# Mixer weights split once, kept in memory, and loaded as pairs by the later blocks of a hybrid encoder block

## The chip, the cores and the metric

One core of one Trainium2 chip runs the whole kernel. The metric is the device time of one execution in microseconds (us). Engines: PE is TensorE, DVE VectorE, ACT ScalarE, POOL GpSimd, SP SyncE, which only issues DMAs here.

## What is computed

One layer of a streaming encoder on 4096 frames of width 1024, in float32, with 16 meta tokens ahead of them:

```python
h = layernorm(concat([meta, x]), ln0)
proj = h @ w_in                      # q k v, conv cb cc ch, gates ga gc
y_attn = window_attention(q, k, v, sinks) @ w_attn_out
y_conv = (cb * conv3(cc * ch)) @ w_conv_out
mix = (sigmoid(ga) * y_attn + sigmoid(gc) * y_conv) @ w_o
h = layernorm(alpha * h + mix, ln1)
h = layernorm(alpha * h + top2_of_32_experts(h), ln2)
```

The change is in the mixer, which is the part up to `mix` and `ln1`.

## The kernel before

**Float32 by halves.** A float32 product on PE is made of three products of rounded parts: high by high, high by low, low by high (`product`, lines 826 to 828). So each weight needs a high part, `w_hi`, and a low part, `w_lo`.

**Blocks and strips.** The mixer works through 8 blocks of 512 frames (`BLOCKS`), one pass of a loop on every engine for each. A block is 50 strips (`N`); a strip is 128 x 1024 weights, 512 KB. Their order is the list `strips` (lines 85 to 90): k, v, four q (strips 0 to 5), then cc, ch, cb four times (6 to 17), then ga, gc, out eight times (18 to 41; `MIX0` is 18), then eight of w_o (42 to 49). Each strip is 24 matmuls of 512 columns. Between the strips PE does the attention of the block (in strips 6 to 15), the router of the block before it (18 to 24) and transposes.

**The way of a strip's weights.** SP loads it into `raw`, which has five places (`load`, line 451: it waits for `lo_ready`, that is for the split of the strip that had the place, so it runs some four strips ahead of the other engines). ACT rounds it to `w_hi` (`split_hi`, line 513), when PE has done with the place of `w_hi`; DVE subtracts to get `w_lo` (`split_lo`, line 656); PE waits for `lo_ready` and multiplies. `w_hi` and `w_lo` have two places each. All this is done again in each of the 8 blocks.

**Counts.** PE adds 1 to `strip_done` at the last matmul of each strip (`mm.then_inc(strip_done, 1)`), and DVE adds 2 at the start (`v.sem_inc(strip_done, 2)`). So `strip_done >= b * N + s + 3` means that strip s of block b is finished.

**The outputs.** Each strip writes one of two banks of PSUM (`pj`) in turn; an out strip writes both, one after the other. PE waits for `pj_taken` before it writes a bank again. ACT empties those of ga and gc (`take`), DVE those of out (lines 764 to 775): line 767 the first bank, line 769 the second.

**The input rows of the next block.** `x_rows` has four tiles of 128 frames. In SP's program a tile's load is issued at steps 26 to 29 (`X_AT`, `MIX0 + 8 + i`), behind the weight load of the same step (line 473). In DVE's program the wait for the tile and its statistics (`measure`, lines 41 to 44) are at steps 26, 29, 32 and 35 (`LN0_AT`), ahead of all else of that step:

```python
X_AT = {MIX0 + 8 + i: i for i in range(TILES)}
LN0_AT = {MIX0 + 8 + 3 * i: i for i in range(TILES)}
...
if s in LN0_AT:
    v.wait_ge(x_in[LN0_AT[s]], b * 16 + 16)
    measure(b * LNS + TILES + LN0_AT[s], LN0_AT[s], xs)
```

At steps 1 to 4 DVE does the statistics of ln1 on the rows of the block before, POOL scales them, and SP stores them at steps 4 to 7, twice (`h1`, 512 KB each).

After the mixer come the routing and the experts, which the change leaves alone.

Of the kernel before, what the change touches and what calls it, by code (L numbers as in the profile page):

```python
# [12 lines left out]
P = 128  # L13
# [40 lines left out]
def mixer(nc, t, x, w_in, w_attn_out, w_conv_out, w_o, h1, logits):  # L54
# [37 lines left out]
    RAW = 5  # L92
    assert N % RAW == 0 and N % 2 == 0
# [35 lines left out]
    with ExitStack() as ctx:  # L129
# [6 lines left out]
        raw = sb("raw", [P, RAW, D])  # L136
        w_hi = sb("w_hi", [P, 2, D], F32R)
        w_lo = sb("w_lo", [P, 2, D], F32R)
# [34 lines left out]
        arena = sb("arena", [P, 2 * KD * TOK])  # L173

        def place(at, name, shape, dt=FP32):
            size = 4 * math.prod(shape[1:])
            assert at[0] + size <= shared + 4 * 2 * KD * TOK
            placed = nc.alloc_sbuf_tensor_at(name, shape, dt, offset=at[0])
            at[0] += size
            return placed  # L180

# [27 lines left out]
        with ExitStack() as c1, nc.Block() as block:  # L209
# [4 lines left out]
            raw_in = [sem1(f"meta_raw_in{i}") for i in range(RAW)]  # L214
# [20 lines left out]
            @block.sync  # L235
            def _(sp):
                def load_strip(n):
                    for dst, src in strip_dmas(*meta_strips[n], raw[:, n % RAW, :]):
                        sp.dma_start(dst, src).then_inc(raw_in[n % RAW], 16)
# [6 lines left out]
                for n in range(1, RAW):  # L246
# [12 lines left out]
                for n in range(RAW, len(meta_strips)):  # L259
                    sp.wait_ge(pj_ready, n - RAW + 1)  # L260
                    load_strip(n)
                sp.wait_ge(consts_in, 16 * (7 + TAPS))
# [104 lines left out]
            @block.tensor  # L367
            def _(pe):
                pe.wait_ge(ident_ready, 1)
                pe.wait_ge(ln_done, 1)  # L370
                for k in range(KD):
                    mm = pe.transpose(tp[0][:, k * META:(k + 1) * META], hm[:, k * P:(k + 1) * P],
                                      ident[0:META, 0:META])
                mm.then_inc(tp_ready, 1)
                uses = [0] * RAW
                for what, n in order:
                    if what == "rows":
                        pe.wait_ge(ln_done, n + 1)
                        for half in range(2):
                            q = 2 * (n - 1) + half  # L380
                            pe.wait_ge(tp_taken_dve, max(1, q))
                            for k in range(4):
                                mm = pe.transpose(tp[q % 2][:, k * P:(k + 1) * P],
                                                  xs[:, n - 1, (4 * half + k) * P:(4 * half + k + 1) * P], ident[:, :])
                            mm.then_inc(tp_ready, 1)
                        continue
                    kind, i = meta_strips[n]
                    uses[n % RAW] += 16 * len(strip_dmas(kind, i, raw[:, 0, :]))
                    pe.wait_ge(raw_in[n % RAW], uses[n % RAW])
                    if n == 0:  # L390
                        pe.wait_ge(tp_taken_dve, 1)
                    if n >= 2:
                        pe.wait_ge(pj_taken, n - 1)
                    for k in range(KD):
                        mm = pe.matmul(pj[n % 2][:, 0:META], raw[:, n % RAW, k * P:(k + 1) * P], hmT[:, k, :],
                                       start=(k == 0), stop=(k == KD - 1))
                    mm.then_inc(pj_ready, 1)
# [4 lines left out]
        h1_out = [sem(f"h1_out{i}") for i in range(TILES)]  # L402
        hi_ready = sem("hi_ready")
# [37 lines left out]
        def raw_uses(s, b):  # L441

            per = lambda ss: 16 * len(strip_dmas(*strips[ss], raw[:, 0, :]))
            slot = s % RAW
            in_block = sum(per(q) for q in range(slot, N, RAW))
            return b * in_block + sum(per(q) for q in range(slot, s + 1, RAW))

        with nc.Block() as block:
            @block.sync
            def _(sp):  # L450
                def load(s, b):

                    hold(sp, lo_ready, b * N + s + 1)
                    for dst, src in strip_dmas(*strips[s % N], raw[:, s % RAW, :]):
                        sp.dma_start(dst, src).then_inc(raw_in[s % RAW], 16)

                load(0, 0)
                with sp.Fori(0, BLOCKS) as b:
                    for s in range(N):
                        load(s + 1, b)  # L460
# [7 lines left out]
                        if s in X_AT:  # L468
# [4 lines left out]
                            sp.dma_start(xs[:, i1, :], x[bass.ds(nxt * TOK + i1 * P, P), :]).then_inc(x_in[i1], 16)  # L473
                for i1 in range(TILES):
# [37 lines left out]
            def _(a):  # L512
                def split_hi(b, s):
                    uses = raw_uses(s, b) if s < N else raw_uses(0, b + 1)
                    a.wait_ge(raw_in[s % RAW], uses)
                    a.wait_ge(strip_done, b * N + s + 1)
                    a.activation(w_hi[:, s % 2, :], raw[:, s % RAW, :], ACT.Copy).then_inc(hi_ready, 1)  # L517
# [30 lines left out]
                split_hi(0, 0)  # L548
                with a.Fori(0, BLOCKS) as b:
                    for s, (kind, i) in enumerate(strips):  # L550
# [30 lines left out]
                        split_hi(b, s + 1)  # L581
# [15 lines left out]
                        if s in HX_AT:  # L597
# [4 lines left out]
                             .then_inc(hx_hi, 1)  # L602
                for i in range(TILES):
# [6 lines left out]
            def _(v):  # L610
# [19 lines left out]
                def take_logits(b, block_of):  # L630
# [7 lines left out]
                v.sem_inc(lo_ready, RAW)  # L638
# [5 lines left out]
                v.wait_ge(hi_ready, 1)  # L644
                v.tensor_tensor(w_lo[:, 0, :], raw[:, 0, :], w_hi[:, 0, :].bitcast(FP32), ALU.subtract)\
                 .then_inc(lo_ready, 1)
                with v.Fori(0, BLOCKS) as b:
# [7 lines left out]

                    def split_lo(s):
                        v.wait_ge(hi_ready, b * N + s + 1)
                        v.tensor_tensor(w_lo[:, s % 2, :], raw[:, s % RAW, :], w_hi[:, s % 2, :].bitcast(FP32),  # L658
                                        ALU.subtract).then_inc(lo_ready, 1)
# [18 lines left out]
                    for s, (kind, i) in enumerate(strips):  # L678
# [29 lines left out]
                        if 0 <= n < UNITS:  # L708
# [24 lines left out]
                        split_lo(s + 1)  # L733
# [68 lines left out]
                    assert steps[0] == DVE_STEPS  # L802
                v.wait_ge(wo_taken, BLOCKS * 2 * TILES + 1)
# [19 lines left out]
            def _(pe):  # L823
# [35 lines left out]
                with pe.Fori(0, BLOCKS) as b:  # L859
                    pe.wait_ge(hx_lo, b * 2 * TILES + 1)  # L860
                    for s, (kind, i) in enumerate(strips):
# [27 lines left out]
                        pe.wait_ge(lo_ready, b * N + RAW + s + 1)  # L889
# [3 lines left out]
                        if kind == "wo":  # L893
# [5 lines left out]
                            for tt in range(TILES):  # L899
# [3 lines left out]
                                for k in range(2):  # L903
                                    w = slice(k * TOK, (k + 1) * TOK)
                                    mm = product(quad[tt][:, :], mT_hi[:, 2 * kk + k, toks], mT_lo[:, 2 * kk + k, toks],
                                                 w_hi[:, s % 2, w], w_lo[:, s % 2, w],
# [5 lines left out]
                        else:  # L912
# [4 lines left out]
                            for part, (x_hi, x_lo, k0, ks) in enumerate(parts):  # L917
                                no = out_no[(s, part)]
                                pe.wait_ge(pj_taken[no % 2], b * (NOUT // 2) + no // 2 + 1)
                                for k in range(ks):  # L920
                                    w = slice((k0 + k) * P, (k0 + k + 1) * P)
                                    mm = product(pj[no % 2][:, :], w_hi[:, s % 2, w], w_lo[:, s % 2, w],
# [54 lines left out]
                        if s in HX_AT:  # L977
# [8 lines left out]
                            mm.then_inc(hx_ready, 1)  # L986
                pe.wait_ge(hx_lo, BLOCKS * 2 * TILES + 1)
# [677 lines left out]
```

## Time and profile before

| | us |
|---|---|
| three runs | 4330.54, 4335.98, 4336.49 |
| median | 4335.98 |
| the profiled execution, its own time | 4333.28 |
| its span, first to last instruction | 4331.5 |
| of this the mixer's 8 blocks, 62 to 2691 us | 2629 |
| PE busy over the span | 4171.0 (96%) |
| DVE busy | 2518.7 (58%) |
| ACT busy | 1773.0 (41%) |

The difference between 4333.28 and 4331.5 is what lies around the span. Matmuls are pipelined: a row gives 390 to 400 ns for one of 512 columns, but they start some 227 ns apart. PEld is PE's weight load, which overlaps. "Idle before" is the time that the engine stood still ahead of such an instruction, and what ended it; "issue" means that nothing in the profile ended it. SPq is SP's queue, where DMAs are issued. Where two rows of DVE seem to overlap by some 0.1 us, the end of the first is its last write.

### The profile page before, as it was taken

The page shows a single profiled execution, that of the slowest core. Times are in us where ns is not written, and L with a number is a line of the kernel's source. Part 1 is how long each engine was busy: PE and PEld are TensorE (multiplying, and loading weights), DVE is VectorE, ACT ScalarE, POOL GpSimd, SP SyncE. Part 2 cuts the span into 40 slices and gives each one's busy share as a digit, 9 for nine tenths or more (in the row PEclk, how much of TensorE's full clock was granted, in tenths as well). Part 3 has the DMA queues.
Part 4 walks back from the last instruction along what each step waited for, and adds up shares of the span by engine and source line. Part 5 has one row for each costly group of instructions (what it writes and reads, how often), then busy time and mean ns, then how long its engine had stood idle before and what let it go on. Part 6 is the DMA issues. An engine that isn't in the chain of part 4 may idle for free. (4 is left out here: it accounts for less than half of the span.)

```text
span 4331.5 us, 62892 instructions
## 1 busy us (share of the span) xinstructions
PE 4171.0 (96%) x20252; PEld 3428.8 (79%) x20253; DVE 2518.7 (58%) x3263; ACT 1773.0 (41%) x2950; POOL 1094.6 (25%) x1117
## 2 busy tenths in 40 slices
PE   7999999999999999999999999499999999999997
PEld 7887887887887888888888887388788888778886
DVE  5555555555555655645645645777666666765664
ACT  2422422422422422422422422466555555654553
POOL 4022032022022021121121121134333333333333
PEclk9999999999999999999999999799999999999998
DMA  6333333333333333333332332187666666765562
GB/s 171 85 107 103 93 102 98 99 104 97 102 104 89 107 106 85 107 104 89 111 102 80 117 102 78 54 289 248 246 199 198 206 199 234 251 203 198 194 204 90
DMA packets 569472, 601.49 MB, mean 139 GB/s; under 512 B 104080, under 2 KB 426640, under 8 KB 569248
## 3 DMA queue, kind: packets, MB, share of 16 engines
q1 hardware_dynamic: 521152, 476.88, 35.5%
q0 software_dynamic: 48096, 121.71, 8.4%
q8 instruction: 130, 2.13, 0.2%
q14 instruction: 94, 0.77, 0.1%
HBM read 527.15 MB, written 124.78 MB: 151 GB/s over the span
## 5 line engine op out<-in xcount | busy, mean ns | idle before, releaser
L826 PE MATMUL bank<-hT_hi,w_hi 128*128 128x512 f32 x2176 | 864.8, 397 | 30.1 <-DVE w_lo L658 21.3
L658 DVE TENSOR_TENSOR w_lo<-raw,w_hi 128x1024 fp32r<-128x1024 f32 x400 | 597.3, 1493 | 485.5 <-ACT w_hi L517 484.4
L827 PE MATMUL bank<-hT_lo,w_hi 128*128 128x512 f32 x2176 | 850.6, 391 | 2.4 <-issue 2.4
L828 PE MATMUL bank<-hT_hi,w_lo 128*128 128x512 f32 x2176 | 849.2, 390 | 0.0
L1565 PE MATMUL e_bank<-e_w_hi,e_xT_hi 128*128 128x512 f32 x1312 | 521.9, 398 | 14.2 <-DVE e_xT_lo L1488 12.4
L826 PEld LDWEIGHTS bank<-hT_hi,w_hi 128*128 128x128 f32 x2176 | 408.9, 188 | 140.4 <-DVE w_lo L658 32.6
L1567 PE MATMUL e_bank<-e_w_hi,e_xT_lo 128*128 128x512 f32 x1312 | 514.3, 392 | 0.0
L1566 PE MATMUL e_bank<-e_w_lo,e_xT_hi 128*128 128x512 f32 x1312 | 513.4, 391 | 0.0
L1493 DVE TENSOR_TENSOR e_w_lo<-e_raw,e_w_hi 128x1024 fp32r<-128x1024 f32 x384 | 444.4, 1219 | 117.7 <-ACT e_w_hi L1441 110.8
L828 PEld LDWEIGHTS bank<-hT_hi,w_lo 128*128 128x128 f32 x2176 | 408.9, 188 | 87.4
L827 PEld LDWEIGHTS bank<-hT_lo,w_hi 128*128 128x128 f32 x2176 | 409.3, 188 | 86.6 <-issue 5.4
L517 ACT ACTIVATE w_hi<-raw 128x1024 fp32r<-128x1024 f32 x401 | 421.1, 1050 | 12.5 <-PE bank L828 7.9
L1441 ACT ACTIVATE e_w_hi<-e_raw 128x1024 fp32r<-128x1024 f32 x384 | 374.7, 1054 | 18.6 <-DMA e_raw<-in_w_exp_gate_dram 11.1
L1565 PEld LDWEIGHTS e_bank<-e_w_hi,e_xT_hi 128*128 128x128 f32 x1312 | 248.0, 189 | 67.4 <-issue 18.0
L1567 PEld LDWEIGHTS e_bank<-e_w_hi,e_xT_lo 128*128 128x128 f32 x1312 | 247.8, 189 | 53.4
L49 POOL TENSOR_SCALAR rstd<-moments 128x1 f32<-128x1 f32 (+1 forms) x73 | 43.5, 596 | 968.6 <-DVE moments L44 968.6
L1566 PEld LDWEIGHTS e_bank<-e_w_lo,e_xT_hi 128*128 128x128 f32 x1312 | 248.3, 189 | 49.7
L503 POOL COPY h_rows<-x_rows 128x1024 f32<-128x1024 f32 x32 | 33.4, 1044 | 986.7 <-PE bank L838 986.7
L1565 PE MATMUL e_bank<-e_w_hi,e_aT_hi 128*128 128x512 f32 x664 | 266.6, 401 | 2.8 <-DVE e_both L1502 2.7
L1567 PE MATMUL e_bank<-e_w_hi,e_aT_lo 128*128 128x512 f32 x664 | 260.2, 392 | 0.0
L1566 PE MATMUL e_bank<-e_w_lo,e_aT_hi 128*128 128x512 f32 x664 | 259.6, 391 | 0.0
L540 ACT ACTIVATE work<-bank 128x512 f32<-128x512 f32 x128 | 76.6, 599 | 427.6 <-PE bank L828 427.6
(277 smaller groups left out, 7173.3 us busy)
## 6 DMA issues: line engine op xcount, KB each, us to landing
raw<-in_w_in_dram SPq DMA_DIRECT2D x251, 512.0 KB, 3.9
e_raw<-in_w_exp_gate_dram SPq DMA_DIRECT2D x128, 512.0 KB
e_raw<-in_w_exp_up_dram SPq DMA_DIRECT2D x128, 512.0 KB
e_raw<-in_w_exp_down_dram SPq DMA_DIRECT2D x128, 512.0 KB
h_rows<-h_rows SPq DMA_DIRECT2D x72, 512.0 KB, 3.5
raw<-in_w_o_dram SPq DMA_DIRECT2D x64, 512.0 KB, 3.8
raw<-in_w_in_dram SPq DMA_DIRECT2D x64, 256.0 KB, 3.7
raw<-in_w_attn_out_dram SPq DMA_DIRECT2D x64, 256.0 KB, 2.8
```

Source lines behind the costliest of these rows:

```text
L49: po.tensor_scalar(rstd[0:rows, :], moments[0:rows, 1:2], LN_EPS, None, ALU.add).then_inc(ln_rstd, 1)
L517: a.activation(w_hi[:, s % 2, :], raw[:, s % RAW, :], ACT.Copy).then_inc(hi_ready, 1)
L540: a.activation(w[:, 0:TOK], got, ACT.Sigmoid).then_inc(taken_act, 1)
L658: v.tensor_tensor(w_lo[:, s % 2, :], raw[:, s % RAW, :], w_hi[:, s % 2, :].bitcast(FP32), ALU.subtract).then_inc(lo_ready, 1)
L826: pe.matmul(out, hi, x_hi, start=first, stop=False)
L827: pe.matmul(out, hi, x_lo, start=False, stop=False)
L828: return pe.matmul(out, lo, x_hi, start=False, stop=last)
L1441: a.activation(w_hi[:, c, :], raw[:, c, :], ACT.Copy).then_inc(split_count(e, c, True)[0], 1)
L1493: v.tensor_tensor(w_lo[:, c, :], raw[:, c, :], w_hi[:, c, :].bitcast(FP32), ALU.subtract)\
L1565: pe.matmul(out_p, hi, x_hi, start=first, stop=False)
L1566: pe.matmul(out_p, hi, x_lo, start=False, stop=False)
L1567: return pe.matmul(out_p, lo, x_hi, start=False, stop=last)
```

## The change

Block 0 is written out ahead of the loop, and the loop runs over blocks 1 to 7. In block 0 each strip is split as before, but two strips ahead, into one of three slots that hold high and low parts together (1 MB); SP stores the slot to memory (`split_weights`, 50 MB). `raw` has three places there. In blocks 1 to 7 SP loads strips from that tensor into four slots, three strips ahead, and nothing is split. SP's step s waits for `strip_done` there, where it waited for `lo_ready`. The rest of SP's step, the stores of h1 and the loads of x, stays behind that wait. The branch for block 0 in DVE's program goes, and a wait for `mlo_ready` comes in at the out strips.

```diff
-    RAW = 5
+    RAW, META_RAW = 3, 5
+    SLOTS = 4
+    ahead = RAW
+    slot_of = list(range(SLOTS)) * 5 + [0, 1, 2] + list(range(SLOTS)) * 6 + [0, 1, 2]
+    def first_slot(s):
+        return (s + 1) % RAW
...
-                def load(s, b):
-                    hold(sp, lo_ready, b * N + s + 1)
-                    for dst, src in strip_dmas(*strips[s % N], raw[:, s % RAW, :]):
+                def load_raw(s):
+                    if s >= RAW:
+                        sp.wait_ge(lo_ready, s - RAW + 1)
+                    for dst, src in strip_dmas(*strips[s], raw[:, s % RAW, :]):
                         sp.dma_start(dst, src).then_inc(raw_in[s % RAW], 16)
...
+                def store_split(s):
+                    sp.wait_ge(lo_ready, s + 1)
+                    sp.dma_start(split_d[s], slots[first_slot(s)]...).then_inc(w_out[first_slot(s)], 16)
+                def load_split(s, b):
+                    sp.wait_ge(w_out[first_slot(s)], ...)
+                    sp.dma_start(slots[slot_of[s]]..., split_d[s]).then_inc(w_in[slot_of[s]], 16)
...
-                load(0, 0)
-                with sp.Fori(0, BLOCKS) as b:
+                def block_of_loads(b, first):
                     for s in range(N):
-                        load(s + 1, b)
+                        if first:
+                            store_split(s)
+                        if first and s + ahead < N:
+                            load_raw(s + ahead)
+                        else:
+                            hold(sp, strip_done, b * N + s + 3)
...
+                            load_split((s + ahead) % N, b + (s + ahead) // N)
                         if s - 3 in LN1_AT:
...
                         if s in X_AT:
...
                             sp.dma_start(xs[:, i1, :], x[bass.ds(nxt * TOK + i1 * P, P), :]).then_inc(x_in[i1], 16)
...
-                        split_hi(b, s + 1)
+                        if first and s + 2 < N:
+                            split_hi(s + 2)
...
-                            if n == 1:
-                                with v.If(b == 0):
-                                    v.tensor_copy(bias[0:CHUNK, :, META:PREV], bias_prev[:, :, :])\
-                                     .then_inc(prev_set, 1)
+                            if n == 1 and first:
+                                v.tensor_copy(bias[0:CHUNK, :, META:PREV], bias_prev[:, :, :]).then_inc(prev_set, 1)
                                 v.wait_ge(prev_set, 1)
...
-                        split_lo(s + 1)
+                        if first and s + 2 < N:
+                            split_lo(s + 2)
...
+                            if i or not first:
+                                v.wait_ge(mlo_ready, b * KD + i)
...
-                        pe.wait_ge(lo_ready, b * N + RAW + s + 1)
+                        if first:
+                            pe.wait_ge(lo_ready, s + 1)
+                            w_of = slots[first_slot(s)]
+                        else:
+                            pe.wait_ge(w_in[slot_of[s]], w_uses(s, b))
+                            w_of = slots[slot_of[s]]
```

On ACT, DVE and PE the body of the loop becomes a function too, called once for block 0 and once in a loop from 1 to `BLOCKS`.

## Rows read from the trace of the kernel before

**Rows 1.** Stretches of one block: PE, PEld, DVE, ACT, POOL busy, clock, DMA, GB/s
```profile
core 0: us, PE busy (x) PEld busy (x) DVE busy (x) ACT busy (x) POOL busy (x), PEclk, DMA share, GB/s
62.00:391.00 329.00, 325.23 (x1611) 267.59 (x1612) 179.31 (x241) 108.98 (x198) 60.13 (x36) 1.00 0.37 104
...
2362.00:2691.00 329.00, 324.54 (x1612) 266.10 (x1612) 179.77 (x242) 106.23 (x196) 60.99 (x36) 1.00 0.31 92
```

**Rows 2.** Costliest groups of the page: busy us, mean ns, idle before
```profile
L658 DVE TENSOR_TENSOR w_lo<-raw,w_hi 128x1024 fp32r<-128x1024 f32 x400 | 597.3, 1493 | 485.5 <-ACT w_hi L517 484.4
L517 ACT ACTIVATE w_hi<-raw 128x1024 fp32r<-128x1024 f32 x401 | 421.1, 1050 | 12.5 <-PE bank L828 7.9
```

**Rows 3.** Waits of PE and PEld from 60 to 2730 us: total, times, longest
```profile
PE bank L826 <- DVE w_lo L658: 21.3, 20, 1.3
...
PEld bank L826 <- DVE w_lo L658: 32.6, 31, 1.6
```

**Rows 4.** Order of time, PE at strip 7 and DVE at a block's start
```profile
1094.58 0.50 PE L826 MATMUL bank<-hT_hi,w_hi 128*128 128x512 f32 x1 [1.26 <-DVE w_lo L658]
...
1379.66 0.20 DVE L676 COPY kT<-kT 128x64 f32<-128x64 f32 x1 [2.25 <-issue]
```

**Rows 5.** Order of time, PE between strips 26 and 27, DVE and ACT behind strips
```profile
1246.17 0.40 PE L828 MATMUL bank<-zT_hi,w_lo 128*128 128x512 f32 x1
1246.41 0.40 PE L826 MATMUL bank<-hT_hi,w_hi 128*128 128x512 f32 x1
...
1246.61 0.69 DVE L769 TENSOR_TENSOR work<-bank,work 128x512 f32<-128x512 f32 x1 [2.04 <-PE bank L828]
...
1252.09 0.60 ACT L540 ACTIVATE work<-bank 128x512 f32<-128x512 f32 x1 [2.44 <-PE bank L828]
1257.53 0.60 ACT L540 ACTIVATE work<-bank 128x512 f32<-128x512 f32 x1 [3.89 <-PE bank L828]
```

**Rows 6.** DMA queues of the page: packets, MB, share; and the 40 slices
```profile
q1 hardware_dynamic: 521152, 476.88, 35.5%
q0 software_dynamic: 48096, 121.71, 8.4%
...
GB/s 171 85 107 103 93 102 98 99 104 97 102 104 89 107 106 85 107 104 89 111 102 80 117 102 78 54 289 248 246 199 198 206 199 234 251 203 198 194 204 90
```

**Rows 7.** First matmuls of strips 4 and 8 of block 3, order of time
```profile
1071.72 0.39 PE L826 MATMUL bank<-hT_hi,w_hi 128*128 128x512 f32 x1
...
1102.05 0.50 PE L826 MATMUL bank<-hT_hi,w_hi 128*128 128x512 f32 x1
```

**Rows 8.** Order of time, SP's queue, steps 26 and 27 of block 3
```profile
1210.41 0.37 SPq L455 DMA_DIRECT2D raw<-in_w_in_dram  x1
1211.20 0.95 SPq L473 DMA_DIRECT2D x_rows<-in_x_dram  x1
1218.78 0.37 SPq L455 DMA_DIRECT2D raw<-in_w_in_dram  x1
1219.48 0.36 SPq L473 DMA_DIRECT2D x_rows<-in_x_dram  x1
```

**Rows 9.** Order of time, DVE at step 26 of block 3
```profile
1237.67 0.69 DVE L41 BATCH_NORM_STATS2 stats<-x_rows 128x6 f32<-128x512 f32 x1
1238.27 0.68 DVE L42 BATCH_NORM_STATS2 stats<-x_rows 128x6 f32<-128x512 f32 x1
1239.05 0.21 DVE L44 BATCH_NORM_AGGREGATE moments<-stats 128x2 f32<-128x12 f32 x1
...
1243.88 0.69 DVE L767 TENSOR_TENSOR work<-bank,work 128x512 f32<-128x512 f32 x1
```

**Rows 10.** DMA issues of the page's answer: KB each, us to landing
```profile
raw<-in_w_in_dram SPq DMA_DIRECT2D x251, 512.0 KB, 3.9
x_rows<-in_x_dram SPq DMA_DIRECT2D x32, 512.0 KB, 4.8
x_rows<-in_x_dram SPq DMA_DIRECT2D x1, 2048.0 KB, 11.8
```

**Rows 11.** Order of time, PE behind the 7.51 us that precede block 0
```profile
62.66 0.79 PE L826 MATMUL bank<-hT_hi,w_hi 128*128 128x512 f32 x1 [7.51 <-DVE w_lo L645]
...
66.66 0.44 PE L826 MATMUL bank<-hT_hi,w_hi 128*128 128x512 f32 x1
66.94 0.39 PE L827 MATMUL bank<-hT_lo,w_hi 128*128 128x512 f32 x1
```

**Rows 12.** Order of time, PE behind a shorter gap in the experts
```profile
3054.03 1.12 PE L1611 MATMUL e_bank<-e_ident,e_prod 128*128 128x128 f32 x4 [2.62 <-DVE e_prod L1542]
```

**Rows 13.** The stretch behind that gap, columns as in rows 1
```profile
3054.00:3060.20 6.20, 5.48 (x14) 4.20 (x15) 5.95 (x7) 6.20 (x8) 1.65 (x2) 0.50 0.49 163
```

More of the change, by code:

```diff
@@ L91, in mixer @@
     N = len(strips)
-    RAW = 5
-    assert N % RAW == 0 and N % 2 == 0
+    RAW, META_RAW = 3, 5
+    SLOTS = 4
+    ahead = RAW
+    slot_of = list(range(SLOTS)) * 5 + [0, 1, 2] + list(range(SLOTS)) * 6 + [0, 1, 2]
+    assert N == len(slot_of)
+    def first_slot(s):
+        return (s + 1) % RAW
     CONV0 = 2 + PAIRS
@@ L134, in sem @@
             return ctx.enter_context(nc.semaphore(name))
-        raw = sb("raw", [P, RAW, D])
-        w_hi = sb("w_hi", [P, 2, D], F32R)
-        w_lo = sb("w_lo", [P, 2, D], F32R)
+        split_d = nc.dram_tensor("split_weights", [N, P, 2 * D], FP32).ap()
         xs = sb("x_rows", [P, TILES, D])
@@ L180, in place @@
             return placed
+        at = [weights]
+        slots = [place(at, f"w_slot{i}", [P, 2, D], F32R) for i in range(SLOTS)]
+        raw = place([weights + 4 * 6 * D], "raw", [P, RAW, D])
+        meta_raw = place([weights + 4 * 4 * D], "meta_raw", [P, META_RAW, D])
         at = [shared]
@@ L213, in mixer @@
             gains_in = sem1("gains_in")
-            raw_in = [sem1(f"meta_raw_in{i}") for i in range(RAW)]
+            raw_in = [sem1(f"meta_raw_in{i}") for i in range(META_RAW)]
             ln_step, ln_moments, ln_rstd, ln_gained, ln_done = (
@@ L237, in load_strip @@
                 def load_strip(n):
-                    for dst, src in strip_dmas(*meta_strips[n], raw[:, n % RAW, :]):
-                        sp.dma_start(dst, src).then_inc(raw_in[n % RAW], 16)
+                    for dst, src in strip_dmas(*meta_strips[n], meta_raw[:, n % META_RAW, :]):
+                        sp.dma_start(dst, src).then_inc(raw_in[n % META_RAW], 16)
                 sp.dma_start(hm, t["meta"]).then_inc(meta_in, 16)
@@ L245, in _ @@
                 sp.dma_start(xs[:, :, :], x[0:TOK, :].rearrange("(t p) d -> p t d", p=P)).then_inc(x_in, 16)
-                for n in range(1, RAW):
+                for n in range(1, META_RAW):
                     load_strip(n)
@@ L258, in _ @@
                     sp.dma_start(dst, row.unsqueeze(0).to_broadcast([P, row.shape[0]])).then_inc(consts_in, 16)
-                for n in range(RAW, len(meta_strips)):
-                    sp.wait_ge(pj_ready, n - RAW + 1)
+                for n in range(META_RAW, len(meta_strips)):
+                    sp.wait_ge(pj_ready, n - META_RAW + 1)
                     load_strip(n)
@@ L374, in _ @@
                 mm.then_inc(tp_ready, 1)
-                uses = [0] * RAW
+                uses = [0] * META_RAW
                 for what, n in order:
@@ L387, in _ @@
                     kind, i = meta_strips[n]
-                    uses[n % RAW] += 16 * len(strip_dmas(kind, i, raw[:, 0, :]))
-                    pe.wait_ge(raw_in[n % RAW], uses[n % RAW])
+                    uses[n % META_RAW] += 16 * len(strip_dmas(kind, i, meta_raw[:, 0, :]))
+                    pe.wait_ge(raw_in[n % META_RAW], uses[n % META_RAW])
                     if n == 0:
@@ L394, in _ @@
                     for k in range(KD):
-                        mm = pe.matmul(pj[n % 2][:, 0:META], raw[:, n % RAW, k * P:(k + 1) * P], hmT[:, k, :],
+                        mm = pe.matmul(pj[n % 2][:, 0:META], meta_raw[:, n % META_RAW, k * P:(k + 1) * P], hmT[:, k, :],
                                        start=(k == 0), stop=(k == KD - 1))
@@ L402, in mixer @@
         h1_out = [sem(f"h1_out{i}") for i in range(TILES)]
+        w_in = [sem(f"w_in{i}") for i in range(SLOTS)]
+        w_out = [sem(f"w_out{i}") for i in range(RAW)]
         hi_ready = sem("hi_ready")
@@ L439, in mixer, with raw_uses, w_uses @@
         LNS = 2 * TILES
[L441 to L446, printed above, removed]
+        def raw_uses(s):
+            return sum(16 * len(strip_dmas(*strips[q], raw[:, 0, :])) for q in range(s % RAW, s + 1, RAW))
+        def w_uses(s, b):
+            slot = slot_of[s]
+            return 16 * ((b - 1) * slot_of.count(slot) + slot_of[0:s + 1].count(slot))
         with nc.Block() as block:
@@ L473, in _ @@
                             sp.dma_start(xs[:, i1, :], x[bass.ds(nxt * TOK + i1 * P, P), :]).then_inc(x_in[i1], 16)
+                for s in range(ahead):
+                    load_raw(s)
+                block_of_loads(0, True)
+                with sp.Fori(1, BLOCKS) as b:
+                    block_of_loads(b, False)
+                for s in range(ahead):
+                    sp.wait_ge(w_in[slot_of[s]], w_uses(s, BLOCKS))
                 for i1 in range(TILES):
@@ L512, in _, with split_hi @@
             def _(a):
[L513 to L517, printed above, removed]
+                def split_hi(s):
+                    a.wait_ge(raw_in[s % RAW], raw_uses(s))
+                    if s >= RAW:
+                        a.wait_ge(strip_done, s - RAW + 3)
+                        a.wait_ge(w_out[first_slot(s)], 16 * (sum(first_slot(q) == first_slot(s) for q in range(s))))
+                    a.activation(slots[first_slot(s)][:, 0, :], raw[:, s % RAW, :], ACT.Copy).then_inc(hi_ready, 1)
                 def take(b, s):
@@ L546, in take_rows, with block_of_strips @@
                      .then_inc(rt_act, 1)
-                split_hi(0, 0)
-                with a.Fori(0, BLOCKS) as b:
+                def block_of_strips(b, first):
                     for s, (kind, i) in enumerate(strips):
@@ L602, in _ @@
                              .then_inc(hx_hi, 1)
+                for s in range(2):
+                    split_hi(s)
+                block_of_strips(0, True)
+                with a.Fori(1, BLOCKS) as b:
+                    block_of_strips(b, False)
                 for i in range(TILES):
@@ L643, in _, with split_lo, block_of_strips @@
                 v.sem_inc(hx_lo, 1)
[L644 to L647, printed above, removed]
+                def split_lo(s):
+                    slot = slots[first_slot(s)]
+                    v.wait_ge(hi_ready, s + 1)
+                    v.tensor_tensor(slot[:, 1, :], raw[:, s % RAW, :], slot[:, 0, :].bitcast(FP32),
+                                    ALU.subtract).then_inc(lo_ready, 1)
+                def block_of_strips(b, first):
                     steps = [0]
@@ L802, in _ @@
                     assert steps[0] == DVE_STEPS
+                for s in range(2):
+                    split_lo(s)
+                block_of_strips(0, True)
+                with v.Fori(1, BLOCKS) as b:
+                    block_of_strips(b, False)
                 v.wait_ge(wo_taken, BLOCKS * 2 * TILES + 1)
@@ L857, in router_logits, with block_of_strips @@
                     mm.then_inc(lg_ready, 1)
-                with pe.Fori(0, BLOCKS) as b:
+                def block_of_strips(b, first):
                     pe.wait_ge(hx_lo, b * 2 * TILES + 1)
@@ L887, in _ @@
                             mm.then_inc(s_ready, 1)
[L889 removed]
+                        if first:
+                            pe.wait_ge(lo_ready, s + 1)
[3 more added lines that the diff above has]
+                            w_of = slots[slot_of[s]]
                         if kind == "out" and i == 0:
@@ L986, in _ @@
                             mm.then_inc(hx_ready, 1)
+                block_of_strips(0, True)
+                with pe.Fori(1, BLOCKS) as b:
+                    block_of_strips(b, False)
                 pe.wait_ge(hx_lo, BLOCKS * 2 * TILES + 1)
```

20 lines of the change are left out of this document (12 added, 8 removed).

## The prediction

> **What bounds the kernel now.** I read the stretches of single blocks first, since the change touches only the mixer. A block takes 329 us and PE is busy for 325 of them, at the full granted clock; DVE is busy for 179, ACT for 108, and the DMA engines move about 100 GB/s [rows 1]. Every one of the 8 blocks looks like this. So the mixer is bound by PE, and less work for DVE and ACT is worth only what PE waits for them. The costliest groups say that the splits are 597.3 us of DVE and 421.1 us of ACT [rows 2]; those are the large numbers of this change, and nearly all of them lie beside PE. The waits say what does not: PE stood still for `w_lo` 20 times in the mixer, 21.3 us in all, and its weight load 31 times, 32.6 us [rows 3]. These are some 3 or 4 places in each block: strip 1, where DVE is late because its loop begins again, strip 5 behind the layernorm work, and strip 7, where the split stands behind the preparation of the first scores (1.26 us in the row) [rows 4].
>
> **What is taken away.** In blocks 1 to 7 no `w_lo` is made, so these waits go; in block 0 the split is made two strips ahead, which gives it a strip of 5.44 us more (the two ends of ga and gc strips in [rows 5] are that far apart), and the waits are 1.6 us at most. Matmul rows overlap (0.39 us for one that starts every 0.23), so the PE figure is short by up to 0.16 us a time and the PEld figure holds some of its normal gaps. I take the middle, **27 us gained**, with 21.3 and 32.6 as ends. What could be late next at these places is DVE's preparation of scores or ACT's exponentials; both come sooner once their engines split nothing, so I take nothing off. The other 7/8 of 597.3 and 421.1 us are worth 0: PE's own work hides them.
>
> **Block 0.** SP now moves 0.5 MB in and 1 MB out for each strip; over a block of 329 us that is 79 MB or 240 GB/s, and slices at 248 and 289 GB/s stand in the page [rows 6]. A store has two strips and a raw load three before anyone needs it, so I take 0 (up to 10 us if that cover fails once). `raw` has three places for five, which is still three strips of lead. In block 0 SP's step waits for a split that is made two steps ahead of DVE's own step, so its loads of x are early enough.
>
> **The loads of blocks 1 to 7.** 1 MB for each strip of 5.44 us or more is at most 193 GB/s. The bytes that a busy DMA system moves follow from the queues: 476.88 MB in 35.5% of 4331.5 us is 310 GB/s for the mixed packets of q1, and 121.71 MB in 8.4% is 334 GB/s for the large ones of q0 [rows 6]. At 334 GB/s a slot of 1.05 MB takes 3.1 us, and its load is issued when PE ends strip s for use at strip s + 3, two strips or 10.9 us later. So the weights arrive in time: 0. At steps 4 to 7 two stores of 0.5 MB are behind each load, 2.1 MB or 6.3 us a strip; strips 4 to 7 together take PE 30.3 us, from 1071.72 to 1102.05 [rows 7], which is more than 4 times 6.3: 0.
>
> **What is moved: the loads of x.** This is the large term. SP's step 26 issues the weight load and then tile 0 of x. Today it is released by a split far back: in block 3 x was issued at 1211.20 [rows 8] and DVE measured it at 1237.67 [rows 9], 26 us later. After the change step 26 waits for `strip_done >= b * N + 29`, which is the end of strip 26 itself. But DVE's step 26 begins with the wait for that very tile, and only behind it, in order, comes line 767, which empties the first bank of strip 26. PE needs this bank for strip 27. So PE comes to a stop at the end of strip 26 until x has been asked for, has landed and has been measured. Nothing deadlocks, since strip 26 itself needs only what ACT has emptied. The length:
> - from the end of strip 26 to SP's first issue 0.1 us, as DVE follows the last matmul of strip 26 (1246.17 and 0.40) by less than that [rows 5].
> - from that issue to x landed: today x is issued 0.70 to 0.79 us behind the raw load [rows 8] and lands 4.8 us later [rows 10], 5.6 together, with 0.52 MB of small pieces ahead of it. I put a slot there instead: take away 0.52 MB at the mixer's own rate (104 GB/s at a share of 0.37 is 281 GB/s [rows 1]: 1.9 us) and add 3.1: 6.8 us.
> - the statistics, from 1237.67 to 1239.26, 1.6 us, then line 767, 0.69 us [rows 9], and 0.1 for the step to PE.
> - PE's next strip starts now 0.16 us before the last matmul's modelled end (1246.41 against 1246.57) [rows 5]: 0.2.
>
> That is 0.1 + 6.8 + 1.6 + 0.7 + 0.1 + 0.2 = **9.5 us in each of 7 blocks, 66.5 us**. Lower end: the slot ahead costs no more than raw did, and x lands as it does now: 8.0. Upper end: the 2 MB load with a strip ahead of it took 11.8 us [rows 10], about 2 of latency and 0.27 MB a us; at that rate 1.57 MB take 5.8, and with 3 us of latency for it all the stop is some 11.5.
>
> A page that gives a price for this is the Trainium skill's "DMA: Bandwidth & Descriptors", section "Anatomy of one DMA": some 2.0 us fixed and the bytes at 436 GB/s. By it the slot and x would land 5.6 us after the issue and the total would be about 8 us lower than mine; no row here moves bytes at that rate.
>
> **The clock.** Behind the 7.51 us ahead of block 0 nine matmuls start 0.44 us apart, from 62.66 to 66.66, where the next follow at 0.23 to 0.28 [rows 11]: half speed, 1.2 of 2.4 GHz. In the experts a gap of 2.62 us was enough for a stretch of 6.20 us at a granted clock of 0.50 [rows 12, 13], while the gaps of up to 1.3 us in the mixer left it at 1.00 [rows 1, 3]. A stop of 9.5 us is above both, so strip 27 starts at half speed: 4.0 us that would be 2.0, **2 us in each of 7 blocks, 14 us**. Ends: 0, and 3.1 (half of 6.20).
>
> **The second tile.** Tile 1 is issued at the end of strip 27 and waited for at DVE's step 29. It is measured 0.1 + 6.8 + 1.6 = 8.5 us after that end and line 767 is done at 9.2; PE needs the bank at the start of strip 30, 11.1 us after it. So 0, with 1.9 us of slack; at the upper end of the landing 0.1 to 0.5 each. Tiles 2 and 3 have 3 and 5 strips more.
>
> **Small things together.** The wait for `mlo_ready` is for DVE's own work of three strips before: 0. Three loads at the end that no one uses lie beside the last layernorm: 0 to 1 us. The program of the mixer gets twice as long, and one jump back is saved. At a jump DVE idles 2.25 us for "issue" [rows 4], beside PE's work. I take 0. By the Trainium skill, "Runtime: NRT & Kernel Launch", section "Instruction fetch mechanics", a straight program is fetched ahead and a taken branch stalls; by that rule the sum would be about 1 us lower, and the longer program free. No run here shows it.
>
> **Sum.** -27 + 66.5 + 14 = +53.5 us. On the profiled execution's 4333.3 that gives 4386.8; the median of the runs is 2.7 above that execution, so **4390 us**.
>
> **Rivals.**
> (1) *x is in time.* PE doesn't stop, because SP gets past step 26 before the end of that strip. It decides at about 9.5 us ahead of that end; a release by strip 25 would leave half the stop, 7 times 4, and end near 4336. In full it gives 4336 - 27 = 4309, faster. For it: the step was harmless before, with 26 us to spare. Against it: the count says strip 26, and DVE's order is fixed. 0.07.
> (2) *The slots come late.* If stores and loads at steps 4 to 7 ran at 200 GB/s, as in many slices of the experts [rows 6], 8.4 MB would take 42 us where PE takes 30.3 [rows 7]; less the lead of 6 to 7 that is some 5 us a block, 35 on top: 4425. Were the rate poor throughout, every strip would pay. Against it: 248 and 289 GB/s in the same row, and DMA was under 0.4 busy in the mixer. 0.07.
> (3) *The waits for `w_lo` turn into others* (scores, `qT`), and nothing is gained: 4417. 0.06.
> The forecast has 0.80.
>
> **Range.** Low: 7 x 8.0 - 32.6 = +23, no loss by the clock: 4360. High: 7 x (11.5 + 3.1 + 0.3) - 21.3 = +83, 4420; a little of rival 2 added, 4424. Both contain rival 3. A measurement can tell about 0.2%, 9 us, from no change: between 4327 and 4345 lies only a half-hidden stop, 0.02; faster 0.08, slower 0.90.
>
> **What would show it.** Right: in blocks 1 to 7 one idle time of 9 to 10 us on PE ahead of the first matmul of strip 27, put down to line 767 of DVE, with DVE idle before the statistics of x and ended by the DMA of x; half-speed matmuls behind it; blocks 1 to 7 some 8 us longer than now and block 0 some 3 shorter; no wait of PE for weights. Wrong: blocks 1 to 7 shorter than 328 us, a PE wait for a slot's DMA, or the stop at strip 30 as well.

## The result, and the profile after

The changed kernel takes 4385.4 us (median of 4, 4379.77 to 4390.03), the kernel before in the same session 4333.26 (4330.43 to 4336.49): a ratio of 1.012, interval 1.0102 to 1.0137. It is slower by 52 us, as forecast (4390, range 4360 to 4424).

The page of the changed kernel, its costliest groups (busy us, mean ns, idle before) and its issues (KB, us to landing):

```profile
L884 PE MATMUL bank<-hT_hi,w_slot 128*128 128x512 f32 x2176 | 871.1, 400 | 76.8 <-DVE work L819 60.7
...
w_slot<-split_weights SPq DMA_DIRECT2D x353, 1024.0 KB, 4.8
...
x_rows<-in_x_dram SPq DMA_DIRECT2D x32, 512.0 KB, 5.4
```

Stretches of block 0 and block 3, columns as in [rows 1]:

```profile
62.00:388.60 326.60, 325.36 (x1612) 268.55 (x1613) 178.08 (x240) 105.04 (x195) 58.63 (x36) 1.00 0.80 258
1062.80:1398.20 335.40, 324.96 (x1613) 267.88 (x1613) 103.72 (x191) 60.42 (x147) 49.46 (x36) 0.99 0.49 176
```

DVE's work in a block fell from 179 us to 104 and ACT's from 108 to 60, as the change means it to. PE's busy time did not move, and the block is 335.4 us long where it was 329 [rows 1]. The group of line 884 tells why: `w_lo` is gone from what ended PE's idle time [rows 3], and in its place stands line 819, DVE's product that empties the first bank of an out strip (767 in the kernel before). The waits of PE from 60 to 2730 us:

```profile
PE bank L884 <- DVE work L819: 60.7, 8, 9.0
PE bank L884 <- issue: 7.3, 6, 1.3
PE bank L884 <- DVE w_slot L700: 7.1, 1, 7.1
...
PE bank L884 <- DMA w_slot<-split_weights: 1.8, 1, 1.8
```

The third row is the start of the stage and was there before. Order of time at the end of strip 26 of block 3, with what ended each idle time:

```profile
1256.17 0.40 PE L886 MATMUL bank<-zT_hi,w_slot 128*128 128x512 f32 x1
1256.65 0.32 SPq L485 DMA_DIRECT2D w_slot<-split_weights  x1
1257.39 0.34 SPq L512 DMA_DIRECT2D x_rows<-in_x_dram  x1
1262.75 0.69 DVE L41 BATCH_NORM_STATS2 stats<-x_rows 128x6 f32<-128x512 f32 x1 [16.94 <-DMA x_rows<-in_x_dram]
...
1264.36 0.69 DVE L819 TENSOR_TENSOR work<-bank,work 128x512 f32<-128x512 f32 x1
...
1265.10 0.79 PE L884 MATMUL bank<-hT_hi,w_slot 128*128 128x512 f32 x1 [8.54 <-DVE work L819]
1265.69 0.63 PE L885 MATMUL bank<-hT_lo,w_slot 128*128 128x512 f32 x1
...
1268.25 0.47 PE L885 MATMUL bank<-hT_lo,w_slot 128*128 128x512 f32 x1
1268.56 0.39 PE L886 MATMUL bank<-hT_hi,w_slot 128*128 128x512 f32 x1
```

This is the whole of the loss in one place. SP issues the slot at 1256.65, when strip 26 is done, and x at 1257.39; in the kernel before DVE measured x 26 us after its issue [rows 8, 9]. PE stands for 8.54 us, and its first matmuls then start 0.43 us apart, not 0.23.

Beside these views I worked out how long each strip lasts, from the start of its first matmul to that of the next strip's, block by block in both traces. The sums over the 8 blocks, changed kernel less kernel before:

```
strip 26 (the stop)                     +61.9 us
strip 27 (half speed)                   +14.7
strips 4, 5, 6, 13 (waits for w_lo)     -24.2
strips 0, 1, 2, 49 (edges of a block)    +0.4
the other 40                             -1.0
all 50                                  +51.8
```

(A wait at the start of strip 5 counts in the length of strip 4, and so on.) Blocks 1 to 6, from the first matmul of one to that of the next, are 336.4 us long on the mean, where they were 328.4, and block 0 is 326.4 for 329.0. The stretch behind the mixer varied by some 10 us either way between the profiled runs of this study, whatever the kernel; block lengths repeat to 1 or 2 us, so the readings below go by them first.

### The profile page after: what moved, and what is told of

It reads as the page before. It is cut to its first block and busy times, and to the rows that moved or that the text cites. A ratio compares the mean times of both kernels' runs of the same rounds, so it can differ in the third digit from the quotient of the medians.

```text
span 4381.1 us, 60777 instructions
## 1 busy us (share of the span) xinstructions
PE 4173.6 (95%) x20252; PEld 3443.7 (79%) x20253; DVE 1989.8 (45%) x2912; ACT 1439.5 (33%) x2598; POOL 1020.8 (23%) x1117
## 5 line engine op out<-in xcount | busy, mean ns | idle before, releaser
L884 PE MATMUL bank<-hT_hi,w_slot 128*128 128x512 f32 x2176 | 871.1, 400 | 76.8 <-DVE work L819 60.7
L885 PE MATMUL bank<-hT_lo,w_slot 128*128 128x512 f32 x2176 | 855.7, 393 | 0.0
L886 PE MATMUL bank<-hT_hi,w_slot 128*128 128x512 f32 x2176 | 854.2, 393 | 0.2 <-issue 0.2
L884 PEld LDWEIGHTS bank<-hT_hi,w_slot 128*128 128x128 f32 x2176 | 412.8, 190 | 183.8 <-DVE work L819 63.4
L886 PEld LDWEIGHTS bank<-hT_hi,w_slot 128*128 128x128 f32 x2176 | 412.6, 190 | 88.8
L885 PEld LDWEIGHTS bank<-hT_lo,w_slot 128*128 128x128 f32 x2176 | 413.3, 190 | 82.0
L49 POOL TENSOR_SCALAR rstd<-moments 128x1 f32<-128x1 f32 (+1 forms) x73 | 28.2, 386 | 1048.7 <-DVE moments L44 1048.7
L819 DVE TENSOR_TENSOR work<-bank,work 128x512 f32<-128x512 f32 x64 | 44.3, 692 | 361.3 <-PE bank L886 360.9
L884 PE MATMUL bank<-w_slot,mixT_hi 128*128 128x512 f32 x512 | 205.8, 402 | 0.0
```

The costliest lines, as they stand in the source:

```text
L884: pe.matmul(out, hi, x_hi, start=first, stop=False)
L885: pe.matmul(out, hi, x_lo, start=False, stop=False)
L886: return pe.matmul(out, lo, x_hi, start=False, stop=last)
```

## Experiments

**Is it the late x, and is it all of it?** The loads of x four steps earlier in SP's program:

```diff
-        X_AT = {MIX0 + 8 + i: i for i in range(TILES)}
+        X_AT = {MIX0 + 4 + i: i for i in range(TILES)}
```

> The changed kernel with SP's loads of x at steps 22 to 25 instead of 26 to 29. Theory (PE stops because x is asked for only at the end of strip 26, and DVE waits for x ahead of emptying the bank): the stop of some 8.8 us and the half-speed matmuls behind it, some 2 us, go in 7 blocks, 76 us in all: about 4309 us, blocks 1 to 7 near 325.5 us each. Rival (the time is lost to the doubled weight traffic or the longer program, and the stop only shows up at this place): above 4370 us, with idle time of PE elsewhere.

Measured: 4305.67 us, ratio to the kernel before 0.9951 (0.9935 to 0.9968). Blocks 2 to 6 are 325.2 to 325.4 us long. Line 819 is gone from PE's waits:

```profile
PE bank L884 <- issue: 7.1, 6, 1.3
PE bank L884 <- DVE w_slot L700: 7.0, 1, 7.0
...
PE bank L884 <- DMA w_slot<-split_weights: 1.9, 1, 1.9
```

One number in SP's program is worth 80 us by the medians, where 76 were expected, and 74.4 us by the lengths of the blocks. The rest of the change does gain.

**How much earlier?** The same with `MIX0 + 7 + i`, one strip earlier than in the changed kernel:

> The changed kernel with SP's loads of x one step earlier, at steps 25 to 28. Theory: the stop is shorter by exactly one out strip, 5.6 us, so 3.2 us remain in each of 7 blocks: 4385 - 39 = 4346 us if the clock falls to half speed all the same, 4332 us if it holds over 3.2 us. Rival (traffic or program): no change, about 4385 us.

Measured: 4335.13 us, ratio 1.0007 (0.9996 to 1.0019): no change that can be told. Strip 26 is 3.0 to 3.2 us longer than in the kernel before, 21.5 us in 7 blocks; the theory had 3.2. The time lay between the two values given for the clock, and the trace says why. Order of time for PE in block 1 and in block 2:

```profile
586.00 0.50 PE L884 MATMUL bank<-hT_hi,w_slot 128*128 128x512 f32 x1 [2.87 <-DVE work L819]
586.34 0.40 PE L885 MATMUL bank<-hT_lo,w_slot 128*128 128x512 f32 x1
...
914.31 0.50 PE L884 MATMUL bank<-hT_hi,w_slot 128*128 128x512 f32 x1 [2.93 <-DVE work L819]
...
916.02 0.63 PE L884 MATMUL bank<-hT_hi,w_slot 128*128 128x512 f32 x1
916.45 0.63 PE L885 MATMUL bank<-hT_lo,w_slot 128*128 128x512 f32 x1
```

Idle times of nearly the same length leave the clock up in three blocks (strip 27 longer by 0.1 us) and bring it down in four (by 1.7 to 2.8 us).

**Is it x, or DVE's order?** SP as in the changed kernel; DVE's waits for x and its statistics one step later, behind the emptying of the banks:

```diff
-        LN0_AT = {MIX0 + 8 + 3 * i: i for i in range(TILES)}
+        LN0_AT = {MIX0 + 9 + 3 * i: i for i in range(TILES)}
```

> The changed kernel with SP's loads of x left at steps 26 to 29, but DVE's waits for x and its statistics moved one step later (27, 30, 33, 36), behind the emptying of the banks of the out strip. Theory: x is just as late and nobody minds, since PE waits only for the bank: about 4309 us, as with the early load. Rival (the lateness of x itself delays something further down, the transposes at strips 41 to 48): PE stops there, 4340 us or more.

Measured: 4306.57 us, ratio 0.9942 (0.9923 to 0.9962). DVE still waits for x, 7 times and up to 3.5 us, and PE no longer waits for line 819. So the loss needs both: a late transfer, and in DVE's program the wait for it ahead of something that PE wants.

**The late x alone, in the kernel before.** Weights are split in every block; SP's loads of x are at steps 30 to 33, where SP naturally is at that time, and the first waits for strip 26:

```diff
-        X_AT = {MIX0 + 8 + i: i for i in range(TILES)}
+        X_AT = {MIX0 + 12 + i: i for i in range(TILES)}
...
                             hold(sp, h_copied, b * TILES + i1 + 1)
+                            if i1 == 0:
+                                hold(sp, strip_done, b * N + MIX0 + 8 + 3)
```

> The kernel before, where SP issues tile 0 of x only when strip 26 is finished (its loads of x are at steps 30 to 33, with a wait for the end of strip 26 ahead of tile 0); weights are split in every block as before. Theory: the late x alone makes the loss. No slot is ahead of x in the queue here, but a split of 1.2 us lies between the statistics and the bank: a stop of some 8.9 us and 2 us of half speed in 8 blocks, +87 us on the kernel before, about 4420 us. Rival (the loss needs the traffic of the slots or the new program): about 4335 us.

Measured: 4402.76 us against 4330.52, ratio 1.0172 (1.0155 to 1.0189), +72 us. PE waits for DVE's line 769 (767 before) 8 times, 54.8 us; strip 26 is 56.1 us longer in the 8 blocks and strip 27 18.0. The loss needs no slots, no stored weights and no new program. The size was 15 us off, by the stop: 7.0 us a block, not 8.9. I had let x land as late as behind a load, and with nothing ahead of it x landed 3.0 to 3.3 us after its issue.

**What the slot ahead of x costs.** In the changed kernel, x at the same steps of blocks 1 to 7 but issued ahead of the step's weight load (and behind it in block 0 alone):

```diff
+                            if not first and s in X_AT:
+                                load_x(s, b)
                             load_split((s + ahead) % N, b + (s + ahead) // N)
```

> The changed kernel with x still at steps 26 to 29 of blocks 1 to 7, but issued ahead of the weight load of the step. The landing today is 0.74 us of issue and 5.3 more behind the slot. Theory as predicted (the slot ahead delays x by its bytes): x lands some 4.9 us after the end of strip 26 instead of 6.1, the stop is 7.6 us and the total 4377 us. Rival (the slot ahead costs x only its issue, since the transfers overlap): 0.74 us less in 7 blocks, 4380 us. Either way the stop stays: an answer below 4350 would speak against the order as the cause.

Measured: 4367.51 us, ratio 1.0074 (1.0055 to 1.0093). Strip 26 is 6.2 us longer than in the kernel before, not 8.8. In block 3:

```profile
1254.06 0.34 SPq L492 DMA_DIRECT2D x_rows<-in_x_dram  x1
1254.45 0.42 SPq L485 DMA_DIRECT2D w_slot<-split_weights  x1
...
1257.27 0.69 DVE L41 BATCH_NORM_STATS2 stats<-x_rows 128x6 f32<-128x512 f32 x1 [14.41 <-DMA x_rows<-in_x_dram]
```

x is measured 3.21 us after the first of the two issues, not 6.10: the slot ahead costs 2.9 us in each of 7 blocks, more than twice what was expected. This is the time of its bytes (1.05 MB are 3.0 us at 345 GB/s and 3.1 at 334) and hardly anything more. The transfers follow one another: in block 3 of the changed kernel the packets of the slot start at 1257.61 us, and the first one of x starts at 1260.59, when the last ones of the slot are under way.

**The edge between block 0 and block 1.** Block 0's last two stores wait for nothing but their splits, yet SP's program has them behind waits for the ends of strips 47 and 48. On top of the early x:

```diff
-                        if first:
-                            store_split(s)
+                        if first and s < N - 2:
+                            for q in range(s, N if s == N - 3 else s + 1):
+                                store_split(q)
```

> The version with early x loads, in which block 0's last two stores of split weights are issued at step 47, ahead of the waits for the ends of strips 47 to 49, instead of behind the loads of block 1. Theory: PE's waits for the slots of block 1's strips 2 and 3 (1.9 and 1.7 us there, in the early-x version) come from SP standing for its own late stores; they go: about 4302 us, block 1 as long as blocks 2 to 7. Rival (those loads are late for want of DMA rate): no change, 4306 us.

Measured: block 1 is 325.16 us long for 328.44, and the wait for the slot's DMA is gone, as expected. The median is 4305.85 us (6 runs) for 4305.67, ratio 0.9933 (0.9919 to 0.9948): 3 us are below what the medians can tell.

**Would more traffic bring the slots late?** On top of the early x, a copy of 0.5 MB or 1 MB from memory to memory at each step of blocks 1 to 7:

```diff
+                            if not first:
+                                sp.wait_ge(extra_in[s % 5], 16 * ((b - 1) * 10 + s // 5 + 1))
+                                sp.dma_start(extra_d[s % 5], split_d[s][:, 0:D]).then_inc(extra_in[s % 5], 16)
```

> The early-x version with a further copy of 0.5 MB from memory to memory at each step of blocks 1 to 7, which no one waits for. 1.57 MB for a strip of 5.44 us is 289 GB/s. Theory (slots have margin up to some 334 GB/s): within 5 us of 4306. Rival 2 of the prediction (the margin is thin, slots come late): PE waits for slots, 4330 us or more.

> The same with 1 MB of copy at each step: 2.1 MB a strip, 6.3 us at 334 GB/s, above the 5.44 us of the plain strips and with h1 and x some 334 us a block against 325.5 of PE. Theory: now the slots do come late, PE waits for their DMA, some 9 us a block, about 4370 us. Rival (the DMA system moves more than 334 GB/s): near 4306 us.

Measured: 4322.48 us (ratio 0.9982, 0.997 to 0.9994) and 4333.3 (1.0004, 0.9991 to 1.0017), at 260 and 337 GB/s over a block. Slower than 4306 in both, but not for the reason that either side gave. The waits of PE in the second one:

```profile
PE bank L893 <- issue: 24.5, 6, 5.3
PE bank L893 <- DVE w_slot L709: 7.2, 1, 7.2
...
PE bank L893 <- DMA w_slot<-split_weights: 1.7, 1, 1.7
```

No slot is late save the one at the edge of block 1, with twice the bytes. What grows is "issue", six times, once for each jump back of the loop: from 1.3 us at most (early x, some 180 GB/s) to 2.8 and 5.3; on the mean of the six from 1.2 to 2.6 and 4.1.

That is not all of the loss. Behind these idle times matmuls of strip 0 start 0.43 us apart, half speed, in 5 of 6 blocks with 0.5 MB (idle times of 2.4 to 2.8 us) and in 6 of 6 with 1 MB (3.7 to 5.3). In block 3 with 0.5 MB:

```profile
1043.17 0.68 PE L893 MATMUL bank<-hT_hi,w_slot 128*128 128x512 f32 x1 [2.65 <-issue]
1043.65 0.63 PE L894 MATMUL bank<-hT_lo,w_slot 128*128 128x512 f32 x1
1044.07 0.63 PE L895 MATMUL bank<-hT_hi,w_slot 128*128 128x512 f32 x1
```

Against the early x alone, the six idle times add 8.4 and 17.4 us, and strip 0 becomes 7.8 and 12.9 us longer in sum.

**The jump.** Blocks 1 to 7 written out one behind the other (the same edit on ACT, DVE, PE and SP), on the version with stores first, and once more on that with early x and 1 MB of further copy:

```diff
-                with pe.Fori(1, BLOCKS) as b:
+                for b in range(1, BLOCKS):
                     block_of_strips(b, False)
```

> The version with early x loads and early last stores, with blocks 1 to 7 written out one behind the other on ACT, DVE, PE and SP, so that these engines never jump back. Theory: PE's 1.3 us of unexplained idle time between strips 49 and 0 (put down to issue) is the jump, paid 6 times, with what follows in strip 0: about 8 us less, 4298 us, and block lengths near 324 us. Rival (the gap has to do with the end of a block itself): no change, 4306 us.

> The early-x version with 1 MB of further copy at each step of blocks 1 to 7, blocks written out. With the loop this traffic cost 28 us and PE's idle time sat at the jump, 3.6 to 5.2 us a block, not at the slots. Theory (instructions for the target of a jump are fetched over the same busy DMA engines, and a straight program has them fetched ahead): the loss goes, about 4300 us. Rival (so much traffic slows PE at a block's end anyway): about 4333 us.

Measured: 4286.06 us, ratio 0.9895 (0.9877 to 0.9912), and 4289.29, ratio 0.9908 (0.9891 to 0.9924). PE has no "issue" wait left at a block's edge in either. The stretch of a whole block of the first:

```profile
710.45:1033.99 323.54, 322.85 (x1613) 266.80 (x1612) 103.78 (x190) 60.46 (x147) 49.50 (x36) 1.00 0.52 182
```

A stretch of the other, with 345 GB/s:

```profile
700.00:1030.00 330.00, 329.31 (x1644) 272.11 (x1643) 104.61 (x191) 61.01 (x148) 49.44 (x36) 1.00 0.88 345
```

Its blocks 2 to 6 are 323.54 us long too. So in these kernels the traffic hurts only at the jump. The page has a queue of kind "instruction" (packets, MB, share) among those of the same 16 DMA engines, here of the changed kernel:

```profile
q8 instruction: 120, 1.97, 0.2%
```

The trace's records of single packets show more. At each jump of these loops over stored weights one instruction packet of 16 KB starts 2.7 to 2.9 us ahead of the first matmul behind the jump, and takes 0.9 to 1.0 us, with and without the copy. It starts some 1.5 us before PE's last work ends at 182 GB/s, some 0.2 us before at 260, and on the mean 1.3 us after it at 337. In the written-out versions no packet of 16 KB starts in the 10 us ahead of a block. So as PE's idle time grows this packet starts later, and doesn't take longer. What holds it back was not measured, and the records don't say whose instructions it carries. The medians moved 20 us where the block lengths moved 10; the other 9 or so are behind the mixer, and I can't say what they are.

**Is storing the split weights worth anything?** All blocks written out, all of them loaded raw and split two strips ahead into three slots, nothing stored. The core of the edit on that version (SP's stores and slot loads are gone as well):

```diff
-                        if first and s + 2 < N:
-                            split_lo(s + 2)
+                        if b * N + s + 2 < BLOCKS * N:
+                            split_lo(b * N + s + 2)
```

> All blocks written out, and in every block the weights are loaded raw and split, two strips ahead, into three slots, as the change does in block 0 alone; nothing is stored and loaded back, so DVE and ACT do all 400 splits again. Theory (PE's waits for the split were the only thing that the stored weights could give, and a split two strips ahead takes the same waits away): the same as the unrolled version with stored weights, within 5 us of it, about 4298 us. Rival (the freed time of DVE and ACT is worth something of its own): slower than that one by 10 us or more.

Measured: 4288.85 us, ratio 0.9904 (0.9887 to 0.992), against 4286.06 with stored weights. A block of it:

```profile
711.32:1034.86 323.54, 322.85 (x1613) 266.77 (x1612) 179.83 (x240) 107.23 (x197) 60.09 (x36) 1.00 0.34 101
```

To the hundredth of a us the block is as long, with 76 us more of DVE and 47 more of ACT. The engines' freed time is worth nothing to the mixer.

**And the kernel before, written out:**

```diff
-                with pe.Fori(0, BLOCKS) as b:
+                for b in range(BLOCKS):
```

> The kernel before with its 8 blocks written out on ACT, DVE, PE and SP, nothing else changed. Theory: the 45 us between the kernel before and the version that is unrolled and splits two strips ahead are 24 us of waits for the split at strips 5, 7, 6 and 14, and the rest is the loop's jump (idle time of PE at strips 49 and 0, and DVE late at strip 1 because its loop begins again); so this one gives about 1.5 us a block, 12 us, 4319 us, and the waits at strips 5 and 7 stay. Rival (the jump costs nothing by itself in the kernel before, only beside more DMA traffic): 4331 us.

Measured: 4309.83 us, ratio 0.9953 (0.9936 to 0.9971), where 4319 was expected. Blocks 1 to 6 are 326.47 us long; the waits for `w_lo` at strips 5 and 7 are there still, 1.0 and 1.3 us each:

```profile
PE bank L826 <- DVE w_lo L658: 18.4, 16, 1.3
```

So 326.47 - 323.54 = 2.9 us a block, 23 us in all, is what the waits for the split cost, and about 2 us a block (328.4 - 326.47) is what the loop's edge did, where 1.5 was expected. The median again fell by some 9 us more than the blocks (13 us).

## Why the prediction was right, point by point

- **The sum.** 53.5 us forecast, 51.8 by the lengths of the strips. Part of this closeness is luck: the stop was 4.6 us shorter in sum than forecast and the gain 2.8 us smaller, and the two errors work against each other. Of the 4.6 us between 4390 and 4385.4, 2.7 are a fourth run of the kernel before, which lowered its median.
- **What bounds.** Right. 7/8 of 1018 us of splits went and PE's busy time stayed; the version that splits always is as fast.
- **The stop, 9.5 us in each of 7 blocks, 66.5 us.** Right in place, cause and number; 8.8 us, 61.9 in all. The landing was 0.7 us too long: 0.74 from the slot's issue to x's and 5.33 more, 6.1, where the sum had 6.8. x alone took 0.5 us less than the 3.7 that the sum left for it, and the slot 0.2 less than its 3.1. The steps beside it hold: 0.1 to SP's issue, 1.6 for the statistics, 0.7 for line 819. The lower end of 8.0 us is not what its words give: with no more for the slot than for raw weights, 9.5 - 1.2 is 8.3. It changes the range by 2 us. The 2 us of latency in the upper end stand in no row; in block 3 of the kernel before with a late x, where nothing is ahead of it, the first packet of x starts 1.0 us after the issue, and the landing is told 0.3 us after the end of the last.
- **The slot in front of x.** The same step took 1.2 us as its extra cost over a raw strip. The whole of it is 2.9, which agrees with a slot's 3.1 of transfer. By the price in the Trainium skill's "DMA: Bandwidth & Descriptors", section "Anatomy of one DMA", the slot and x together were estimated at 5.6; measured 6.1, about halfway between this and the sum's 6.8. That section gives its fit for single DMAs that GpSimd issues, and these two were issued by SP.
- **The clock, 2 us a block, 14 us.** Right: 14.7. The rows for it (a stretch behind 7.51 us and one behind 2.62) bracketed the case well; the runs with shorter idle times show that nothing finer could have been said from them, since idle times of 2.9 us went either way, and of those of 2.4 to 2.8 us ahead of strip 0 five in six brought the clock down.
- **The waits for `w_lo`, 27 us.** 24.2 us at the strips where they stood (5, 7, 6 and 14), in all 8 blocks; two written-out versions give 23. The middle of PE's 21.3 and PEld's 32.6 was 3 us too high: the missing part stood at strip 1, and what was gained there went to the jump.
- **The jump, taken as 0.** This is the term that failed, though it was small. The prediction counted DVE's late start at strip 1 among the gains and PE's own jump nowhere. The waits there went, and PE then stood 1.1 to 1.3 us for its own jump in one piece behind strip 49, so strips 0 and 49 together gained 0.8 us in the 8 blocks. The Trainium skill's rule in "Runtime: NRT & Kernel Launch", section "Instruction fetch mechanics" (a taken branch stalls, a straight program is fetched ahead), is what the written-out versions bear out: a block with slots is 325.3 us long in the loop and 323.54 without, 1.7 us a jump, where I had estimated 1 us for the one jump that is saved.
- **The slots in time (rival 2, 0.07).** Ruled out well beyond this traffic. **x in time (rival 1).** Ruled out by the trace. Its half, a release by strip 25, was forecast at 4336 and measured at 4335.13, and that is luck: the stop left was 3.1 us, not 4, and the clock took 8.2 us in 7 blocks that the forecast left out. **Other waits (rival 3).** None came, save at the jump and at the edge of block 1.
- **The edge of block 1.** 2 us that the prediction did not name: SP stands for the landing of its own late stores.
- **The second tile.** Right: x is waited for at step 29 as well, and PE is not.

## What to carry to other kernels

When a load queue is put behind another condition, everything that is issued in that queue moves with it: go through each transfer that it issues and look up who waits for it, and what that engine does only afterwards. Work on an engine that is not the bound is worth the bound's waits and no more; ask first whether making it one step earlier takes the same waits away, before paying for memory traffic. On a bound engine a loop's jump back has a price, and it grows with what the DMA engines are doing.

## What the runs showed of the hardware

- The idle time of PE at the jump of a long loop, mean of six and longest: 1.2 and 1.3 us at some 180 GB/s of traffic, 2.6 and 2.8 at 260, 4.1 and 5.3 at 337, none in a straight program at 345.
- The clock fell to half speed behind idle times of PE of 2.4 to 2.8 us in 5 of 6 cases, of 2.9 to 3.0 us in 4 of 7, of 3.7 to 5.3 us in 6 of 6, and of 6.0 to 9.0 us in all 22.
- x of 512 KB in 4 KB rows landed 3.0 to 3.3 us after its issue with nothing ahead, 5.3 to 5.8 behind a slot of 1 MB issued 0.74 us earlier; its packets start when those of the slot are nearly done.
- The DMA engines moved 345 GB/s over a whole block beside a PE that was never slowed.
